# Strassen products of half size in the feed-forward input of a transformer's second block

## The reference, cut to what matters

```python
D_FF_2 = -(-8 * D_MODEL // (3 * 256)) * 256
...
for l in range(DEPTH):
    ...
    h = rmsnorm(x, norm_ffn_g[l])
    gt, up = jnp.split(h @ w_ffn_in[l], 2, axis=-1)
    x = x + (jax.nn.silu(gt) * up) @ w_ffn_out[l]
```

## Time and profile before

| | us |
|---|---|
| median of three runs | 3093.24 |
| lowest and highest of them | 3089.74 to 3093.58 |
| the profiled execution, device time | 3090.53 |
| its span, first to last instruction | 3088.7 |
| PE busy in it | 3073.3 (100%) |
| DVE, ACT, POOL busy in it | 1577.0, 1076.5, 238.6 |

### The profile page before, as it was taken

The page is one execution under the profiler, slowest core; times in us unless marked ns, Lnnn a source line. Parts: engine busy times, 40 slices in busy tenths (PEclk is TensorE's granted clock), DMA queues, the critical chain, the costliest instruction groups (busy, mean ns, idle before and its releaser), DMA issues.

```text
span 3088.7 us, 36352 instructions
## 1 busy us (share of the span) xinstructions
PE 3073.3 (100%) x15146; PEld 2552.7 (83%) x15146; DVE 1577.0 (51%) x1904; ACT 1076.5 (35%) x1181; POOL 238.6 (8%) x138
## 2 busy tenths in 40 slices
PE   9999999999999999999999999999999999999999
PEld 7798978888888797888888788888888778888887
DVE  7665555553336655555436754544434766443432
ACT  3323344443233434444323332333323342333321
POOL 0002100110000010001001000110100000100100
PEclk9999999999999999999999999999999999999999
DMA  4412312222321131222333122222232313222222
GB/s 172 116 55 82 137 55 96 95 97 107 121 97 69 69 137 55 95 95 95 109 103 97 68 96 97 95 95 96 94 109 91 108 69 109 86 93 108 90 100 96
DMA packets 47564, 297.67 MB, mean 96 GB/s; under 512 B 7075, under 2 KB 7331, under 8 KB 13396
## 3 DMA queue, kind: packets, MB, share of 16 engines
q1 hardware_dynamic: 42336, 285.91, 26.2%
q10 hardware_dynamic: 5108, 10.02, 1.4%
HBM read 291.16 MB, written 4.75 MB: 96 GB/s over the span
## 4 chain that ended last, share of the span: by engine, by line
PE 92%; DVE 4%; ACT 2%; issue 1%; DMA 1%; SPq 0%; POOL 0%; DVEq 0%; ACTq 0%
PE G L461 85%; PE psS L833 1%; PE psS L1060 1%; DVE mxt L1991 1%; DVE wL L1739 1%; PE G L1065 1%; ACT wH L1294 1%; PE psS L1173 0%; PE G L1182 0%; PE psT L558 0%; DVE ws L2559 0%; PE psT L1209 0%; DMA ws<-bias_rows 0%; ACT ws L1394 0%; PE psT L776 0%
## 5 line engine op out<-in xcount | busy, mean ns | idle before, releaser
L461 PE MATMUL G<-hH,wH 128*128 128x512 f32 x2560 | 1014.5, 396 | 4.7 <-DVE wL L2101 2.3
L461 PE MATMUL G<-hH,wL 128*128 128x512 f32 x2560 | 998.2, 390 | 0.0
L461 PE MATMUL G<-hL,wH 128*128 128x512 f32 x2560 | 997.4, 390 | 0.0
L1739 DVE TENSOR_TENSOR wL<-raw,wH 128x2048 fp32r<-128x2048 f32 x259 | 624.2, 2410 | 542.2 <-ACT wH L1294 542.0
L461 PE MATMUL G<-wsr,wH 128*128 128x512 f32 (+1 forms) x2512 | 743.9, 379 | 0.8 <-DVE x L1930 0.2
L1294 ACT ACTIVATE wH<-raw 128x2048 fp32r<-128x2048 f32 x263 | 502.3, 1910 | 675.8 <-PE G L461 656.7
L461 PEld LDWEIGHTS G<-hH,wH 128*128 128x128 f32 x2560 | 481.0, 188 | 117.3 <-issue 15.8
L461 PEld LDWEIGHTS G<-hH,wL 128*128 128x128 f32 x2560 | 480.9, 188 | 102.1
L461 PEld LDWEIGHTS G<-hL,wH 128*128 128x128 f32 x2560 | 481.4, 188 | 97.9 <-issue 1.2
L461 PEld LDWEIGHTS G<-wsr,wH 128*128 128x128 f32 x2512 | 462.5, 188 | 91.4 <-DVE wsr L2383 1.6
L461 PE MATMUL G<-wsr,wL 128*128 128x512 f32 (+1 forms) x1256 | 475.1, 378 | 0.0
(11 more groups left out here) (297 smaller groups left out, 2473.0 us busy)
## 6 DMA issues: line engine op xcount, KB each, us to landing
raw<-in_units SPq DMA_DIRECT2D x263, 1024.0 KB, 4.8
ws<-bias_rows SPq DMA_DIRECT2D x2, 1536.0 KB, 15.2
bias_rows<-ws ACTq DMA_DIRECT2D x1, 2560.0 KB
x<-in_x SPq DMA_DIRECT2D x4, 512.0 KB, 7.9
ws<-in_mem ACTq DMA_DIRECT2D x2, 1024.0 KB, 4.9
ws<-bias_rows ACTq DMA_DIRECT2D x1, 2048.0 KB, 9.1
out_x<-x SPq DMA_DIRECT2D x3, 512.0 KB, 6.8
ws<-in_decay ACTq DMA_DIRECT2D x1, 1280.0 KB, 9.4
```

Source lines behind the costliest of these rows:

```text
L461: mm = pe.matmul(o, mv if swap else wt, wt if swap else mv, start=first and n == 0, stop=last and n == 2)
L1739: V.tensor_tensor(wL[:, g.p, :], raw[:, g.p, :], wH[:, g.p, :].bitcast(F32), ALU.subtract)\
```

## The change

Of the 11 pairs of a layer in the second block, the first three stay as they are (`FIRST_7`), and the other eight are made in another way by new functions `ffn7`. A unit's 8x2 weight tiles are taken as 2x2 blocks of 4 tiles by 1, the normalized x as 2x2 blocks of 4 tiles by 256 tokens, and the product of the two is made from seven products of blocks (Strassen's scheme in its form with few sums) instead of eight. So a unit is 7 products x 4 tiles x 3 passes = 84 matmuls with 256 columns, and the pair 14 products, in an order that mixes gate and up (`PRODUCTS`).

- x has to be normalized ahead of the sums: DVE writes `xn` (8 instructions), POOL makes four sums of x blocks once a layer, ACT and DVE split the seven block operands into high and low parts.
- The weight sums are made per unit by POOL, four instructions of 128x512, in place in `raw`, the first one into the slot of a low part (`wl_raw`).
- ACT rounds (`round_`) and DVE subtracts (`low`) in pieces of 512 columns, one per product; each has a slot of an eighth of `wH` and `wL` (`SLOTS`), and a slot is used again when the product that held it is done (`freed`).
- A product's result goes into one of six PSUM regions of 256 columns, some on top of one another (`INTO`). ACT copies accumulators into `tn` and `sq[:, 1]` (`save`), DVE adds others onto them (`add`), ACT makes the Silu in three parts, DVE the product.
- Hidden pairs stay unrounded in `hidden_raw`, and are split by ACT and DVE from the last pair on; POOL has no part in it any more.
- The loop has six of the eight pairs; the first and last are written out.

The new functions and tables, cut to their core (`behind(idx)` is a piece's place in the order in which pieces are made, `freed(idx)` the number of the product that frees its slot):

```diff
+PRODUCTS = (("g", 1), ("g", 2), ("u", 1), ("g", 5), ("g", 6), ("u", 2), ("u", 5), ("g", 7), ("u", 6), ("g", 4), ("u", 7),
+            ("g", 3), ("u", 3), ("u", 4))
+SLOTS = (1, 2, 3, 0, 4, 5, 7, 6, 1, 2, 4, 3, 5, 6)
+MADE = (0, 1, 3, 2, 4, 5, 7, 6, 8, 9, 11, 10, 12, 13)
...
@@ TensorE @@
+            def seven(first=False):
+                needs = {2: 0, 4: 1, 8: 2, 9: 3, 12: 4}
+                for idx, (of, n) in enumerate(PRODUCTS):
...
+                    if idx == 0:
+                        pe.wait_ge(save7, c.k7.v - 1)
+                    elif idx == 2:
+                        pe.wait_ge(save7, c.k7.v)
+                        pe.wait_ge(add7, c.e7.v - 1)
+                    elif idx == 7:
+                        pe.wait_ge(save7, c.k7.v + 3)
+                    elif idx == 10:
+                        pe.wait_ge(save7, c.k7.v + 6)
+                    elif idx in (4, 8, 9, 12):
+                        pe.wait_ge(add7, c.e7.v + needs[idx])
+                    pe.wait_ge(low7, c.p7.v - NP + behind(idx))
...
+                    for k in range(4):
+                        for m, (w, h) in enumerate(((wH, high), (wH, low), (wL, high))):
+                            mm = pe.matmul(o, piece(w, idx)[:, k, :], h[:, k, :],
+                                           start=(n in (1, 2, 5) and k == 0 and m == 0), stop=(k == 3 and m == 2),
+                                           skip_group_check=True)
+                    mm.then_inc(prod7, 1)
...
@@ TensorE, ahead of the residual @@
+                def hidden(k):
+                    if k == 0:
+                        pe.wait_ge(save7, c.k7.v)
+                        pe.wait_ge(add7, c.e7.v)
...
@@ ScalarE @@
+                def round_(idx, ahead=0):
+                    if idx in (0, 2):
+                        act.wait_ge(raw_in[p], (c.unit.base + (c.unit.off + 2 * at)) * 8 + 16)
+                    if idx in sums_of:
+                        act.wait_ge(sum7, c.s7.v + (8 * at + sums_of[idx]))
+                    act.wait_ge(prod7, c.p7.v + (NP * at + freed(idx)))
+                    ins = activation(piece(wH, idx), operand7(idx), ACT.Copy)
...
+                def save(m):
+                    act.wait_ge(prod7, c.p7.v + (m + 1))
+                    if m == 1:
+                        act.wait_ge(add7, c.e7.v)
+                    elif m == 5:
+                        act.wait_ge(add7, c.e7.v + 1)
...
@@ ScalarE, seven @@
+                    for m in range(NP):
+                        if m in (1, 3, 4, 5, 6, 8, 13):
+                            save(m)
+                        for idx in {0: (7, 6), 1: (8,), 2: (9,), 3: (11,), 5: (10, 12), 8: (13,)}.get(m, ()):
+                            round_(idx)
+                        if not last:
+                            for idx in {9: (0, 1), 10: (3,), 12: (2, 4), 13: (5,)}.get(m, ()):
+                                round_(idx, 1)
...
+                        if m == 9:
+                            act.wait_ge(add7, c.e7.v + 3)
+                            act.wait_ge(prod7, c.p7.v + 10)
+                            activation(sq[:, 0, 1, right], tn[:, 1, right], ACT.Silu)
+                            activation(sq[:, 0, 1, left], REGION["g", 1], ACT.Silu).then_inc(save7, 1)
+                        elif m == 12:
+                            act.wait_ge(add7, c.e7.v + 5)
+                            activation(sq[:, 0, 0, :], tn[:, 0, :], ACT.Silu).then_inc(act_g, 1)
...
@@ VectorE @@
+                def low(idx, ahead=0):
+                    dve.wait_ge(round7, c.p7.v + (NP * ahead - NP + behind(idx)))
+                    if idx in (3, 6):
+                        dve.wait_ge(sum7, c.s7.v + (8 * ahead + (3 if idx == 3 else 7)))
+                    V.tensor_tensor(piece(wL, idx), operand7(idx), piece(wH, idx).bitcast(F32), ALU.subtract)\
+                        .then_inc(low7, 1)
...
+                def add(m):
+                    dve.wait_ge(prod7, c.p7.v + (n + 1))
+                    dve.wait_ge(save7, c.k7.v + saved)
+                    V.tensor_tensor(to[:, t, at], to[:, t, at], REGION[of, r], ALU.add).then_inc(add7, 1)
...
+                def product(dst):
+                    dve.wait_ge(act_g, c.hd.v + 1)
+                    dve.wait_ge(add7, c.e7.v + 6)
+                    dve.wait_ge(save7, c.k7.v + 8)
+                    V.tensor_tensor(dst, sq[:, 1], sq[:, 0], ALU.mult).then_inc(add7, 1)
...
@@ VectorE, seven, with product(dst) behind the loop @@
+                    for m in range(NP):
+                        if m in (2, 6):
+                            add(m - 1)
+                        elif m in (7, 10, 11, 12):
+                            add(m)
...
+                        for idx in {0: (7,), 1: (6,), 2: (8,), 3: (9,), 4: (11,), 6: (10, 12), 8: (13,)}.get(m, ()):
+                            low(idx)
...
+                        if not last:
+                            for idx in {9: (0, 1), 11: (3,), 12: (2, 4), 13: (5,)}.get(m, ()):
+                                low(idx, 1)
...
@@ GpSimd, p = 0 gate, 1 up @@
+                def sums_of(p, s1):
+                    first, second = (1, 2) if p == 0 else (behind(2), behind(5))
...
+                    pool.wait_ge(round7, c.p7.v - NP + first)
+                    minus(s1, a21, a22, ALU.add)
+                    pool.wait_ge(sum7, c.s7.v)
+                    minus(a21, a11, a21)
+                    pool.wait_ge(low7, c.p7.v - NP + first)
+                    minus(a11, s1, a11)
+                    pool.wait_ge(low7, c.p7.v - NP + second)
+                    pool.wait_ge(sum7, c.s7.v)
+                    minus(a12, a12, a11)
```

More of the change, by code:

```diff
@@ L55, with behind, freed @@
 JOBS_1 = (68, 66)
-JOBS_2 = 72
+JOBS_2 = 56
+PAIRS = FT // 2
+FIRST_7 = 3
+MID_7 = PAIRS - FIRST_7 - 2
+PRODUCTS = (("g", 1), ("g", 2), ("u", 1), ("g", 5), ("g", 6), ("u", 2), ("u", 5), ("g", 7), ("u", 6), ("g", 4), ("u", 7),
+            ("g", 3), ("u", 3), ("u", 4))
+SLOTS = (1, 2, 3, 0, 4, 5, 7, 6, 1, 2, 4, 3, 5, 6)
+MADE = (0, 1, 3, 2, 4, 5, 7, 6, 8, 9, 11, 10, 12, 13)
+NP = len(PRODUCTS)
+def behind(idx):
+    return MADE.index(idx) + 1
+def freed(idx):
+    held = [n for n in range(idx) if SLOTS[n] == SLOTS[idx]]
+    return held[-1] + 1 if held else max(n for n in range(NP) if SLOTS[n] == SLOTS[idx]) + 1 - NP
 FILL_V1, FILL_V2, FILL_V3, FILL_O = (0, 1), (2, 3, 5, 7), (9, 11, 13, 15), (18, 22, 26, 30, 34, 36)
@@ L382, in col2 @@
             return pc[:, o:o + n]
-        LAYER = dict(job=JOBS_2, unit=UNITS_2, sq=12, stat=6, bc=6, row=32, rw=16, sm=2, hd=FT // 2, piece=8,
+        SEVEN = PAIRS - FIRST_7
+        LAYER = dict(p7=SEVEN * NP, s7=SEVEN * 8, e7=SEVEN * 7, k7=SEVEN * 8, xt=1, job=JOBS_2, unit=UNITS_2, sq=12, stat=6, bc=6, row=32, rw=16, sm=2, hd=FT // 2, piece=8,
                      lay=1, ar=14, mg=8, mh=4, pv=4)
@@ new lines, in ffn7 @@
+            def ffn7(final=False):
+                first_jobs()
+                for n in range(2 * FIRST_7 - 2):
+                    plain(h_op)
+                seven(first=True)
+                with c.repeat(MID_7, p7=NP, e7=7, k7=8, unit=2):
+                    seven()
+                seven()
+                c.xt.off += 1
+                def hidden(k):
+                    if k == 0:
+                        pe.wait_ge(save7, c.k7.v)
+                        pe.wait_ge(add7, c.e7.v)
+                    if k % 2 == 0:
+                        pe.wait_ge(ffn_ready, c.hd.v + (k // 2 + 2))
+                residual(a_op, operand=hidden, pieces=(range(0, 8), range(8, 16), range(16, 22)), final=final)
+                c.hd.off += FT // 2
@@ L2038, in _ @@
             dve.sem_inc(job_free, 2)
+            dve.sem_inc(prod7, NP)
+            dve.sem_inc(add7, 7)
+            dve.sem_inc(save7, 8)
             dve.sem_inc(ffn_ready, 1)
@@ L2848, in _ @@
             c.sq.off, c.bc.off, c.row.off, c.piece.off = 0, 0, 0, 0
-            for l in c.layers(2, chain=CHAIN_P, job=JOBS_2, stat=6, hd=FT // 2, lay=1, mg=8, mh=4):
+            for l in c.layers(2, chain=CHAIN_P, p7=SEVEN * NP, s7=SEVEN * 8, xt=1, job=JOBS_2, stat=6, hd=FT // 2, lay=1, mg=8, mh=4):
                 rstd(rsb, ST)
@@ L2870, in _ @@
                 rstd(rsb, ST)
-                ffn()
-                c.job.off += 4 + 22 + 4
+                ffn7()
+                c.job.off += 4 + 2 * FIRST_7 + 4
 def _columns(v):
```

248 lines of the change are left out of this document (243 added, 5 removed).

## The result

The changed kernel takes 3188.1 us (median of 4 runs, 3187.6 to 3189.1) against 3093.1 us for the kernel before on the same chip: a ratio of 1.031, 95% interval 1.029 to 1.033. That is slower by 95 us, where 3182 us was forecast. The page of its profile answers to the earlier trace rows: busy us with the share of the span and instructions, then the granted clock in 40 slices.

What follows compares the result with a forecast made beforehand. PE was taken as the bound, busy the whole span. Per layer 6.7 + 6 x 5.0 + 7.5 = 44.2 us, two layers 88.4, on 3090.5 gives 3179, plus 2.7 is 3182; range 3135 to 3215 (about 0.82).

Steps and rivals of the forecast that it cites:

- PE's work, 168 x 0.120 = 20.16 us: Per pair on PE: 168 matmuls of 256 columns at 120 ns, 1.60 us less than the 21.76 before.
- the rival of PE's own queue: Register and wait steps ahead of products cost 1.8 us a looped pair, 22 in all, 3204; chance with longer waits 0.17.
- The exclusion: DVE low parts and product and POOL sums block each other in SBUF: 21.0 us a pair, or some 18.5 with handovers.
- The chain through an inner pair: From the end of product 8 to the next product 8: 25.1 us, PE standing about 4.9; with slow clock 26.7.
- steps 2 to 4: DVE low parts and POOL sums 1 to 7, ahead of the pair's product: 2.49, 3.87 and 5.43 us.
- step 5: DVE's product 1.23, sum 8 blocking low 7, lows 7 and 6, then the add 0.42: 4.31 us.
- The clock step: PE's stand once a pair drops its clock to 1.2 GHz: 1.6 us lost per pair, bounded by 0 and 1.6.
- First pair: First pair of a layer: product 4 starts at about 12.5 us, pair 28.5 with the slow clock, 6.7 more than before.
- Last pair: Last pair of a layer: residual waits for the pair's product, 2.5 us left, with 5.0 that is 7.5 more.
- The clock holds: Rival: PE's clock does not fall, 31.4 us a layer, 63 in all, 3156; chance 0.26.
- Not slower, because DVE and POOL find their gaps: Rival: the chain loses part of its waits and PE is the bound again, 3075 us; chance 0.13.
- Loads: SP's weight loads: the loop through a unit's buffer is 18.1 us, under 20.2, so the load sets nothing.

Runs made afterwards that it cites:

- the last run with the sums on DVE: Changed kernel with the eight weight sums on DVE, ACT and DVE orders mended, and 20 filling matmuls ahead of the residual: 3083.2 us, ratio 0.9972 to before.
- the run without exclusion: Changed kernel with the low parts' second operand read from PSUM instead of SBUF, leaving out the true low parts: 3099.8 us, ratio 1.0028 to before.
- the filled run: Changed kernel with 30 unread matmuls of 256 columns issued by PE ahead of product 4 of each pair: 3153.7 us, ratio 1.0206 to before.

## Why the prediction was right, and where its numbers were off

**PE's work, 168 x 0.120 = 20.16 us.** Right: inner pairs of the last run with the sums on DVE take exactly that. (The formula that the prediction quotes beside it from the Trainium skill, "TensorE: Matmul & The Clock Gate", Back-to-back issue gap, stands there as the gap of isolated matmuls, and not as the rate of a stream with a weight load for each matmul, which this is. The forecast went by the rows and did not use it.) It also settles the rival of PE's own queue: all its wait and register steps are still there and cost nothing that shows.

**The exclusion.** Right, by its rows and by the run that removes it. Low parts took 1069 ns in the mean and POOL's sums 1549 to 1739 by group, against 684 and 1294.

**The chain through an inner pair**, step by step, from the trace: from ACT's copy of product 8 (2103.62) to the next low part 1.77 us (forecast 1.83); from there (2105.39) to the product (2117.14) 11.75 (steps 2 to 4: 11.79); from the product to product 4 (2121.09) 3.95 (step 5: 4.31); from there through products 4 to 8 to the next copy of product 8 9.9 (7.20 and 1.6 for the clock). Sum 27.4, forecast 26.7. Steps 1 to 5 are 0.5 us too long in the forecast, and the clock step is too short.

**The clock step is the term that was mis-sized.** 1.6 us was forecast, from the one fall in before, eight matmuls of 512 columns; it measured 2.39, as the low level lasted longer here and some 25 starts were 0.213 and not 0.12 apart. Beside it each stand costs another 0.25 us that the forecast had not (21.13 = 20.16 + 0.73 + 0.25 in the run without exclusion). The rows give its two parts: a stand is counted from the end of the last matmul, 0.28 us after its start, where the next one would have started after 0.12; and behind a stand the second matmul starts 0.21 us after the first and not 0.12 (2117.33 and 2117.54 in the run with 30 filling matmuls, the third at 2117.66). That is 0.16 + 0.09. In a pair: 20.16 + 3.96 + 0.35 + 2 x 0.25 + 2.39 = 27.36; measured 27.4. An inner pair is 0.5 to 0.6 us longer than the 21.76 + 5.0 of the forecast, 7 us over the twelve.

**First pair.** 28.5 forecast, 28.5 measured in the first layer and 28.0 in the second, but this is luck, two errors that cancel: product 4 started after 11.0 us and not 12.5, so the stand was 5.1 and not 6.7, and the clock fall and the delays behind two stands made up for it.

**Last pair.** The stand ahead of the residual is 2.6 us, 2.5 forecast; the pair 29.8 against 29.3.

**Sum.** 4.2 us more than the 44.2 forecast in the first layer and 3.1 in the second, nearly all from inner pairs: the stretch from the first product to the residual is 222.5 and 221.4 us, and eight pairs were 174.1. The profiled span is 97.3 longer than before, against 88.4 forecast. The forecast of 3182 added 2.7 us for the distance of before's median to its profiled run, which after doesn't have; so the miss in the median is 6 us and not 9.

**Rivals.** The clock holds: refuted by the granted clock and by the filled run. Queue cost: refuted. Not slower, because DVE and POOL find their gaps: refuted for this order; even the best order found with POOL's sums has stands of 1.2 us. Loads: they set nothing, as said.

## What to carry to other kernels

Before you hang a new step on GpSimd beside VectorE's work, add up the instructions of both that read two (VectorE) or any (GpSimd) SBUF operand: if the sum is near the period, treat them as one engine; doing the sums on VectorE alone (0.69 us each instead of 1.3 to 1.7) was faster. Price a stand of TensorE above its own length: here a stand of 4 us cost 4 + 0.25 + 2.4; and look where a clock fall lands, since slow matmuls that only fill another stand cost nothing (24.93 against 24.99 us above). And when an edit removes work from the bounding engine, the gain is only there once every copy and add on the other engines is ordered ahead of whatever waits for something else: the same products and sums ran in 3188 and in 3083 us (3121 with the sums still on GpSimd).

## What the runs showed of the hardware

The length of a stand alone did not settle whether the clock fell. Ahead of the residual PE stood for 2.6 us in the changed kernel and in every variant without a filling there. In the changed kernel the granted clock stayed at 1.00 in both layers and, in the first, the 570 matmuls behind took 129.5 us; in the run without exclusion it fell, and they took 131.05. In the run with the sums on DVE it fell in the first layer (131.10) and not in the second (528 matmuls in 119.97, as in the changed kernel). The row of the chain for the changed kernel, then the stretch of 1 us and the row of the chain for the run without exclusion:

```profile
2277.73 129.48 PE G L538 x570
```

```profile
2234.00:2235.00 1.00, 1.00 (x4) 0.71 (x4) 1.00 (x1) 1.00 (x3) 0.00 (x0) 0.50 0.84 352
```

```profile
2233.57 131.05 PE G L538 x570
```

The stands of 4.0 us were followed by a fall in every inner pair of both layers, those of 1.0 to 1.3 us in none, those of 1.8 to 2.8 in some; what decides between is open. Matmuls that nobody reads kept the clock up at no cost that shows on the other engines (DVE 18.14, ACT 11.49, POOL 13.11 us busy a pair, against 18.12, 11.55 and 13.10): filling 3.6 of the 4.0 us was worth 34 us.
